# Two lanes of the recurrence among smaller weight products, the dilated heads and the mixing after them

## What is computed

```python
z = h @ w_in
za, zb, zc = split(z)                   # a: q, k, v of 12 heads; b: gating; c: recurrence
oa = rmsnorm(dilated_attention(q, k, v, rel_bias_table))      # 12 heads of 64
ob = rmsnorm(u * (causal(w_s) @ layernorm(g) + b_s))          # u, g = gelu(zb)
def step(state, (r_t, w_t, k_t, v_t, kk_t, a_t)):             # c: 12 heads, 256 tokens
    sa = state @ -kk_t
    state = state * w_t + sa * (kk_t * a_t) + v_t * k_t
    return state, state @ r_t
y = concat(oa, ob, oc) @ w_out
x = x + rmsnorm(y)
```

## Time and profile before

| | us |
|---|---|
| median of 3 runs | 2523.7 (2522.8 to 2526.26) |
| the profiled execution | 2520.26 |
| its span in the profile | 2518.5 |
| PE busy, weight loads (PEld) busy | 2323.0 (92%), 2101.7 (83%) |
| DVE, ACT, POOL busy | 1324.9 (53%), 1021.3 (41%), 44.5 (2%) |

### The profile page before, as it was taken

How to read it: one execution, slowest core, us unless ns; L and a number is a source line. 1 busy time by engine, 2 the same in 40 slices (tenths; PEclk the granted TensorE clock), 3 DMA queues, 4 the chain that set the end, 5 groups by cost and what they waited for, 6 DMA issues and landing times.

```text
span 2518.5 us, 35800 instructions
## 1 busy us (share of the span) xinstructions
PE 2323.0 (92%) x14998; PEld 2101.7 (83%) x14998; DVE 1324.9 (53%) x1675; ACT 1021.3 (41%) x1303; POOL 44.5 (2%) x55
## 2 busy tenths in 40 slices
PE   7999988978887899999998999799998999999897
PEld 6898977867766899999997888698976779898676
DVE  5444645375455655555554554644455554444654
ACT  4433432322444544444443344433445443343542
POOL 0000010010000000000000000000000000000000
PEclk9999987979989999999999999899999999999899
DMA  7456520000643455555554555364640546555033
GB/s 283 153 171 213 182 78 1 1 1 19 224 159 101 150 184 182 181 181 181 181 198 159 188 199 186 129 224 156 206 134 1 161 157 222 176 185 167 1 119 132
DMA packets 217831, 373.12 MB, mean 148 GB/s; under 512 B 8263, under 2 KB 108020, under 8 KB 210804
## 3 DMA queue, kind: packets, MB, share of 16 engines
q1 hardware_dynamic: 211088, 360.48, 43.0%
q10 hardware_dynamic: 6628, 10.98, 1.3%
HBM read 369.32 MB, written 2.12 MB: 147 GB/s over the span
## 4 chain that ended last, share of the span: by engine, by line
PE 86%; DVE 8%; ACT 3%; DMA 1%; issue 1%; POOL 0%; ACTq 0%; DVEq 0%; SPq 0%
PE PS L379 25%; PE PS L380 25%; PE PS L381 25%; PE PS L1507 2%; DVE w_lo L321 1%; PE PS L994 1%; PE PS L1491 1%; DVE small L1544 1%; PE PS L1001 1%; ACT w_hi L316 1%; DVE spare L1540 1%; PE PS L574 1%; PE PS L1330 1%; PE PS L1329 1%; PE PS L977 1%
## 5 line engine op out<-in xcount | busy, mean ns | idle before, releaser
L321 DVE TENSOR_TENSOR w_lo<-raw,w_hi 128x2048 fp32r<-128x2048 f32 (+2 forms) x340 | 766.4, 2254 | 788.5 <-ACT w_hi L316 786.5
L316 ACT ACTIVATE w_hi<-raw 128x2048 fp32r<-128x2048 f32 (+2 forms) x340 | 640.3, 1883 | 773.9 <-PE PS L381 756.6
L379 PE MATMUL PS<-h_hi,w_hi 128*128 128x256 f32 x2640 | 750.8, 284 | 5.8 <-DVE w_lo L321 3.6
L380 PE MATMUL PS<-h_lo,w_hi 128*128 128x256 f32 x2640 | 748.1, 283 | 0.0
L381 PE MATMUL PS<-h_hi,w_lo 128*128 128x256 f32 x2640 | 748.0, 283 | 0.0
L379 PE MATMUL PS<-w_hi,h_hi 128*128 128x512 f32 (+2 forms) x1440 | 550.9, 383 | 35.4 <-DVE h_lo L596 12.0
L380 PE MATMUL PS<-w_lo,h_hi 128*128 128x512 f32 (+2 forms) x1440 | 547.5, 380 | 0.0
L381 PE MATMUL PS<-w_hi,h_lo 128*128 128x512 f32 (+2 forms) x1440 | 547.4, 380 | 0.0
L379 PEld LDWEIGHTS PS<-h_hi,w_hi 128*128 128x128 f32 x2640 | 507.9, 192 | 7.8 <-issue 3.9
L380 PEld LDWEIGHTS PS<-h_lo,w_hi 128*128 128x128 f32 x2640 | 508.0, 192 | 0.0
L381 PEld LDWEIGHTS PS<-h_hi,w_lo 128*128 128x128 f32 x2640 | 507.8, 192 | 0.0
(11 more groups left out here) (466 smaller groups left out, 1682.2 us busy)
## 6 DMA issues: line engine op xcount, KB each, us to landing
raw<-in_w_in SPq DMA_DIRECT2D x132, 1024.0 KB, 5.1
raw<-in_ffn_w_up SPq DMA_DIRECT2D x176, 512.0 KB, 4.4
raw<-in_w_out SPq DMA_DIRECT2D x48, 1024.0 KB, 5.1
raw<-in_ffn_w_down SPq DMA_DIRECT2D x44, 1024.0 KB, 4.8
raw<-in_mem_wkv SPq DMA_DIRECT2D x8, 1024.0 KB, 6.9
raw<-in_mem_wq SPq DMA_DIRECT2D x4, 1024.0 KB, 5.4
raw<-in_mem_wo SPq DMA_DIRECT2D x4, 1024.0 KB, 5.2
raw<-in_w_in SPq DMA_DIRECT2D x4, 768.0 KB, 4.5
```

What stands on the lines that cost most here:

```text
L316: act.activation(w_hi[:, slot % 2, :st.n], raw[:, slot, :st.n], ACT.Copy).then_inc(hi_made, 1)
L321: dve.tensor_tensor(w_lo[:, slot % 2, :st.n], raw[:, slot, :st.n], w_hi[:, slot % 2, :st.n].bitcast(F32), ALU.subtract).then_inc(lo_made, 1)
L379: pe.matmul(ps, l_hi, r_hi, start=start, stop=False, skip_group_check=skip)
L380: pe.matmul(ps, l_hi, r_lo, start=False, stop=False, skip_group_check=skip)
```

## The change

1. `b1`, `qk` and `v0` have units of 1024 words: 8 units a group of 256 rows each, 40 in all (`small=True`). A small unit's raw slots are the first half of `raw`, its split slots the first half of each of `w_hi` and `w_lo`. PE does a small unit in two halves with a yield between and after, so the products have 80 steps; ACT and DVE split one unit ahead (`ahead_scalar`, `ahead_vector`).
2. The recurrence has two lanes of three blocks, the second 6 steps later. Both are woven among the 80 product steps, 4 of their steps for each 5. They live in the freed second halves of `raw`, `w_hi`, `w_lo`, in `x` and in `extra`. Every block finishes in its own lane, so a block has 28 steps.
3. The shift moves forward among C (from its third group), C_END and VB (3 steps a unit there). The transposes of the mixing matrices also go among VB. GELU and layernorm of b go among the products after `b1`; the mixing itself, and the 12 heads in three lanes, run after the products together with what is left of the recurrence.
4. Masks and the first small weights are loaded by ACT before C; each later block's by ACT at its start (three DMAs) and after the sigmoids (two). SP loads the first two units of `w_out` when the last split of `v0` is made, and they wait for no lane; ACT and DVE split the first within the last part. `x`, overwritten as scratch, is loaded again among the `w_out` products.

```diff
-        ST_B1 = Stage(count, "b1", w_cols(w_in, 3 * A_W + 256), 1, tok=(0, 512))
+        ST_B1 = Stage(count, "b1", w_cols(w_in, 3 * A_W + 256, kb=2), 1, tok=(0, 512), units=8, kb=2, small=True)
...
+        def ahead_scalar(act, before):
+            for (q, j), n in zip(SMALL_UNITS, range(1, len(SMALL_UNITS) + 1)):
+                if n < len(SMALL_UNITS):
+                    split_hi(act, *SMALL_UNITS[n])
+                if j == 1:
+                    evac_scalar(act, before)
+                yield
+                yield
+                before = q if j == q.st.units - 1 else before
...
-        SHIFTS = (18, 15, 12, 0, 3, 6, 9)
+        SHIFTS = (0, 3, 6, 9, 12, 15, 18)
+        PREPARE = ("d0", "m0", "d3", "m3", "d6", "m6", "d9", "m9", "", "d12", "m12", "d15",
+                   "m15", "v0", "a0", "d18", "m18", "v1", "a1", "v2", "a2", "sigmoid")
...
         def prepare_scalar(act):
...
+            for step in PREPARE:
+                if step[:1] == "a":
+                    n = int(step[1:])
+                    act.wait_ge(prep.pe, prep[f"v{n}"])
...
+        def matrices_tensor(pe):
+            pe.wait_ge(sgu_in, 48)
             for n in range(2):
                 for g in range(4):
-                    last = pe.transpose(PS[:, b, g * P:(g + 1) * P], mix_w[:, 4 * n + g, :], ident[:, :])
+                    last = pe.transpose(PS[:, w_bank(n), g * P:(g + 1) * P], mix_w[:, 4 * n + g, :], ident[:, :])
                 last.then_inc(sgu.pe, 1)
                 yield
                 yield
+
+        def matrices_scalar(act):
+            for n in range(2):
+                yield
+                act.wait_ge(sgu.pe, sgu[f"w{n}"])
...
+            if not j.first:
+                act.wait_ge(j.dve, j.dve0)
+                load_end(act, lane, j.b)
             act.wait_ge(j.pe, j["lora"])
             act.activation(E, PS[:, A, 0:S], ACT.Sigmoid, bias=par("w0", j.b)).then_inc(j.act, 1)
             act.activation(a, PS[:, A, S:2 * S], ACT.Sigmoid, bias=par("a0", j.b)).then_inc(j.act, 1)
+            if j.b + 2 < CB:
+                load_lora(act, lane, j.b + 2)
...
+        LANE_JOBS = [side_jobs[0::3], side_jobs[1::3], side_jobs[2::3] + [a_norm]]
...
-        def mixer(e, recur, side):
-            run(together(*[one_by_one([recur(e, rk_jobs[b]) for b in (i, i + 3)]) for i in range(3)],
-                         *[one_by_one([side(e, j) for j in jobs]) for jobs in LANE_JOBS]))
+        def recurrence(e, recur):
+
+            return together(*[later(6 * i, one_by_one([recur(e, rk_jobs[b]) for b in range(i, CB, 2)])) for i in range(2)])
+        def heads_and_mixing(e, side, mixing, early=iter(())):
+            return together(*[one_by_one([side(e, j) for j in jobs]) for jobs in LANE_JOBS], mixing, early)
+        def with_products(main, fill, gating):
+
+            weave(first(main, 2 * ST_B1.units), fill, 4, 5)
+            fill = together(fill, later(3, gating))
+            weave(main, fill, 4, 5)
+            return fill
...
+            c = products_tensor(pe, ST_C)
+            some(c, 8)
             fill = prepare_tensor(pe)
...
+            weave(c, fill)
+            weave(products_tensor(pe, ST_CE), fill)
+            fill = together(fill, matrices_tensor(pe))
+            weave(products_tensor(pe, ST_VB), fill, 3)
             run(fill)
-            mixer(pe, recur_tensor, side_tensor)
+            fill = with_products(one_by_one([products_tensor(pe, st) for st in SMALL]), recurrence(pe, recur_tensor),
+                                 iter(()))
+            run(together(fill, heads_and_mixing(pe, side_tensor, mixing_tensor(pe))))
 
             mixer_made(pe)
...
+            act.dma_start(xs_(MASKS, 8 * P), I["masks"][:, 0:8 * P]).then_inc(masks_in, 16)
+            act.dma_start(xs_(ENDS, P + 2), I["masks"][:, 9 * P:10 * P + 2]).then_inc(masks_in, 16)
+            act.dma_start(pair_mask, I["pair_mask"]).then_inc(masks_in, 16)
+            for b, lane in enumerate(rk_lanes):
+                load_lora(act, lane, b)
+                load_end(act, lane, b)
...
+            sp.wait_ge(lo_made, ST_V0.U1)
+            for j in range(2):
+                load_unit(sp, Group(ST_OUT, 0), j)
             mixer_made(sp)
+            for j in range(2, 4):
+                load_unit(sp, Group(ST_OUT, 0), j)
             sp.dma_start(gains, bcast("sandwich_gains", D, D)).then_inc(gains_in, 16)
-            products_sync(sp, ST_OUT)
+            products_sync(sp, ST_OUT, range(1, 2))
+            sp.dma_start(x[:, :, :], I["x"][0].rearrange("(t p) d -> p t d", p=P)).then_inc(x_in, 16)
+            products_sync(sp, ST_OUT, range(2, 4))
```

More of the change, by code:

```diff
@@ L96, in together, with some, weave, first @@
         yield
-def weave(main, fill):
-    for _ in main:
-        next(fill, None)
+def some(part, n):
+    for _ in range(n):
+        next(part)
+def weave(main, fill, steps=1, per=1):
+    done = 0
+    for n, _ in enumerate(main, 1):
+        while done < n * steps // per:
+            next(fill, None)
+            done += 1
+def first(part, n):
+    for _ in range(n):
+        next(part)
+        yield
+def later(n, part):
+    for _ in range(n):
+        yield
+    yield from part
 def run(part):
@@ L216, in hybrid_two_blocks @@
         landed = [new(f"landed{j}") for j in range(4)]
+        small_landed = [new(f"small_landed{j}") for j in range(4)]
         right_landed = [new(f"right_landed{j}") for j in range(4)]
@@ L282, in slot_filled @@
             def slot_filled(self, j):
-                return self.plus(8 * self.st.units, 16 * ((self.first + j) // 4 + 1))
+                before = ST_B1.U if self.st.small else SMALL_COUNT if self.first >= ST_V0.U1 else 0
+                return self.plus(8 * self.st.units, 16 * ((self.first + j - before) // 4 + 1))
             def number(self, k):
@@ L1096, in recur_scalar @@
             for c in range(TB):
-                act.activation(two(yt[:, c, bs]), own(B, c), ACT.Copy).then_inc(j.act, 1)
+                act.activation(two(lane["Y"][:, c, :]), own(B, c), ACT.Copy).then_inc(j.act, 1)
             yield
-            if j.inside:
-                yield from finish_scalar(act, j, j, L)
+            yield from finish_scalar(act, j, L)
         def recur_vector(dve, j):
@@ L1444, in side_gpsimd @@
                     yield
-            elif j.kind == "norm":
+            else:
                 yield from attention_norm_gpsimd(pool, j)
-            else:
-                yield from finish_gpsimd(pool, j, j.made, j.lane["var"], j.lane["p"][:, 0:S])
         def heads(lanes, n, name, pairs, scale, v, put, put_steps, bias=None, sink=None, put_act=""):
@@ L2517, in _ @@
                 pool.memset(lane["mats"], 0.0).then_inc(zero.pool, 1)
-            mixer(pool, recur_gpsimd, side_gpsimd)
+            steps = one_by_one([first(iter(range(2 * len(SMALL_UNITS))), 2 * len(SMALL_UNITS))])
+            fill = with_products(steps, recurrence(pool, recur_gpsimd), gating_gpsimd(pool))
+            run(together(fill, heads_and_mixing(pool, side_gpsimd, mixing_gpsimd(pool))))
             add_gpsimd(pool, add_out)
```

532 lines of the change are left out of this document (262 added, 270 removed).

## The result

| | before | after |
|---|---|---|
| median (lowest to highest), us | 2524.9 (2522.8 to 2526.3) | 2590.1 (2589.7 to 2592.0) |
| the profiled execution's span | 2518.5 | 2587.9 |
| PE busy | 2323.0 (92%) | 2347.7 (91%) |
| first product of `b1` | 234.2 | 256.6 |
| last product of `v0` | 350.5 | 563.5 |

The start of `b1` after the change is counted back over the 768 matmuls from `v0`'s last. The same count gives 234.0 before the change, where the prediction has 234.2.

A forecast was written before the change was run, and what follows sets the result against it. PE, busy 92%, was taken as the bound, with 108 us winnable around the mixer. Terms 14 + 220 + 33 + 72 + 25 + 4 = 368 us against 403, 35 less, gave 2489 us; range 2450 to 2528.

The forecast's parts named there:

- ahead of the products: Before `b1`: 14 us of waiting, 3 from C starting late and 11 in VB; bounds 5 and 20.
- among the products: work, waits: Stretch of `b1`, `qk` and `v0` with 64 recurrence steps: 220 us of PE work, 33 of waiting; waiting bounds 10 and 109.
- behind them: After the products, 26 steps with heads and mixing: 72 us of work, 25 of waiting; waiting bounds 12 and 44.
- into `w_out`: From the last lane to the first `w_out` product: 4 us instead of 12, only transposes and their copies remaining.
- so the 12 solve steps hide fully: Doubling steps among the products: 1.4 us of products ahead of each cover DVE's 0.7 and its release 0.2.
- under PE's 6.3 us a unit: Small units' splits on DVE: 40 of 1.2 us in place of 20 of 2.3, costed at nothing.
- the clock should be 1.00 from `b1` to the end of `v0`: Sign to check among the products: PE at full clock throughout, `v0` ending near 501 us.
- Term (a): Among the products, lane two's step 1 waits behind lane one's step 7 on DVE: 4.3 us in each round of 28 steps.
- if the last part runs at half clock: Sign that would prove the forecast wrong: half clock after the last product, a part put at some 97 us to lanes' end.
- every step costs what it does now: Rival: 90 new steps wait 1.7 us each as in the old mixer, 60 us more, 2584; chance 0.10.
- my 0.64: Forecast's waiting in us for each of the 90 recurrence steps, among and after the products: 33 + 25 = 58 us.
- The table switches: ACT's sigmoid/exp switches: skill page's drain, some 11 more switches, 15 us, 2504 if fully on path; forecast assumed no drain.

The follow-up runs named there:

- e15_both_places: Changed kernel with ACT's copy moved ahead of its second step in the unit before and DVE's subtraction between its two steps; 2556.2 us, ratio 1.0130.
- e3_behind: Changed kernel with the recurrence started behind the last product, all 96 steps beside the heads and the mixing; one run, 2610.4 us.
- e12_apart_only: Changed kernel with only the second lane 14 steps behind the first in place of 6; 2565.9 us, ratio 1.0167.
- e11_all: Changed kernel with both splits moved, lanes 14 steps apart, one recurrence step per product step, and VB's transposes and copies staggered; 2517.8 us, ratio 0.9973.
- e14_best_heads: e11_all with the second lane of heads one step and the third two steps behind the first; 2510.4 us, ratio 0.9949 against the kernel before.
- e5_stagger: Changed kernel with the mixing matrices' transposes among C's units and copies of the transposed v one VB unit later; 2574.3 us, ratio 1.0203.
- e13_fill_pause: Changed kernel with 14 useless matmuls on PE ahead of the wait for the normalization's squares, in each of six blocks; 2587.0 us, ratio 1.0243.
- e4_heads_offset: Changed kernel with the second lane of dilated heads begun 2 steps later and the third 4 steps later; 2583.4 us, ratio 1.0244.
- e1_hi_early: Changed kernel with ACT's copy for the next small unit moved into the unit before, DVE's order unchanged; 2578.3 us, ratio 1.0213.

## Why the prediction was wrong

By its own terms:

| | forecast | measured |
|---|---|---|
| ahead of the products | 14 | 22.4 (256.6 less 234.2) |
| among the products: work, waits | 220 + 33 | 306.9 |
| behind them | 72 + 25 | 140.3 |
| into `w_out` | 4 | 3.9 |
| sum | 368 | 473.5 |

*Ahead, right in kind, 8 us short.* PE's two pauses in VB came as forecast (4.43 and 4.81 us against 4.6 and 4.9). But from VB's first subtraction to `b1`'s first product are 40.5 us in place of 24.3, 16 more where I had 11. Some 2.6 of the 5 us over are an estimate for the half clock behind the second pause (half of the 5.3 us from 248.5 to 253.8), which was no term of mine. C and all behind it came 6.4 us late, not 3: the 16 issues took 11.1 us, where I had sized them at 8 from a single one of 0.45. No run moved them.

*Among the products, the step that failed is "so the 12 solve steps hide fully".* I compared half a unit of products (1.4 us) with DVE's 0.7 and its release 0.2, as if DVE were free when PE's product ended. In the order written out, ACT's copy and DVE's subtraction of the next unit stand between the two: 1.05 and 1.23 us. I had costed the splits at nothing, "under PE's 6.3 us a unit": true for the splits, untrue for what is queued behind them. e15_both_places shows 32 us for it.

*The second failed step is the clock.* I wrote "the clock should be 1.00 from `b1` to the end of `v0`". It was 0.91. Of the 53.9 us too much in this stretch, idle time holds 24 (57.1 against 33) and busy time 30 (249.8 against 220). By an estimate, 249.8 × 0.09, 22 of that is the clock; some 7 stay, of which the products hold 2 (113.8 us in e3_behind against 112).

*Term (a) was right in size and wrong in what it stood for.* I gave lane two's step 1 4.3 us; it waits 4.18 (at 292.68, 436.51 and 576.98). But two set-ups side by side cost 23 us by e12_apart_only, not 4.3 a round, and only 8 of them are waits in front of this matmul. How the rest divides between other waits and the clock, the runs don't say.

*Behind the products, 43 us short.* Idle 31.8 against 25; the rest is busy time, 108.5 against 72. At clock 0.82, 20 of it is the clock, by the same estimate. Nine are a size that I had wrong: the scores of three heads take 6.20 us at the full clock (the first row, of e11_all), 2.07 a head, where I took 12 instruction times of 0.111, 1.33. At the half clock they take 11.13 (the second, of the changed kernel):

```profile
553.40:559.60 6.20, 6.20 (x26) 3.75 (x26) 2.28 (x7) 2.10 (x9) 0.00 (x0) 1.00 0.00 1
```

```profile
577.90:589.03 11.13, 11.13 (x25) 6.34 (x26) 1.75 (x7) 3.53 (x10) 1.01 (x1) 0.50 0.00 0
```

I had named this danger ("if the last part runs at half clock") and given it no chance. Some 8 of the busy time have no cause shown.

*Into `w_out`, right*, and the reload of `x` cost nothing: from the first product of `w_out` to the end are 1880.2 us, before 1881.2.

*The rival "every step costs what it does now"* gave 2584 for 0.10 of chance and missed by 6. In its measure: above the 220 and 72 of work there are 86.9 and 68.3 us in 90 steps, 1.72 each, where it said 1.7. Yet the reason it gave, that in-order queues make each lane wait for the other and for the products, is not a law of the kernel: with the same work and nearly the same count of steps, e14_best_heads has 78 us less. I should have given it far more, since its number was measured, slow clock included, and my 0.64 was built from terms that counted some queues and left out the splits in them and the clock.

*The table switches.* By the Trainium skill (ScalarE: Activation LUTs, What ACT_TABLE_LOAD costs) each switch has 1.4 us of drain beside its load. 13 loads of 1.28 us lie in the changed stretch, and in the three whose next activation waited for no other engine it starts 0.01 to 0.02 us after the load's end (543.97 and 545.26 for a sigmoid). The trace still shows no such drain.

What stays open: how the low clock's cost divides from the pauses that come with it. In most runs both moved together. e5_stagger has the changed kernel's idle time among the products at a higher clock and is 5 us shorter there; e13_fill_pause has the higher clock and is no shorter. Both are differences of single executions within the scatter. The single edits were not each tried on the final version, so the single prices hold for the changed kernel and not as shares of the last one's 78 us.

## What to carry to other kernels

When work is woven in between, the time that it hides is not counted on the engine that gets the filler alone. Write down the order on every engine between a product and its answer, and count all that stands there, work that "is hidden anyway" above all: 1.05 and 1.23 us in front of a 0.7 us answer took 32 us here, and moving them by one step gave it back. Two like lanes a few steps apart collide in their costly steps: 14 steps of 28 were 23 us better than 6, the only two distances tried. And a waiting time per step that was measured in the old kernel is the first forecast for the new one; a smaller one has to be earned for every engine's queue.

## What the runs showed of the hardware

Many short pauses come with a low clock, and with it the same work takes longer. Five of the traces whose stretch among the products holds the same 1673 PE instructions show it: idle time, clock and busy time are 57.1, 0.91 and 249.8 us in the changed kernel, 57.3, 0.92 and 246.3 in e4_heads_offset, 57.0, 0.93 and 244.6 in e5_stagger, 49.1, 0.94 and 242.3 in e1_hi_early, 35.0, 0.95 and 235.5 in e15_both_places. The first three have the same idle time at three clocks, so its sum alone does not set the clock. And the clock stayed at 1.2 GHz from 568 to 592 although PE was busy for 19.76 of those 24 us, over half of it with the long scores of the heads; with 14 matmuls of no use (28 instructions) in its first pause it was at 1.2 GHz for 6.4 us, from 571.0, and then back at 2.4 GHz.
